# Two more weight slots for a mixture-of-experts kernel: the one-hot gate tables are replaced by pieces made expert by expert

## What is computed

```
aff   = softmax(h @ w_router)                 # 256 x 16
rows  = the 32 tokens with the largest aff[:, e]
g, u  = h[rows] @ w_gate[e], h[rows] @ w_up[e]    # 1024 x 1024 each
y     = (silu(g) * u) @ w_down[e]             # 1024 x 1024
x[rows] += gate_vector * aff[rows, e] * y
```

## Time and profile before

| | |
|---|---|
| median of 3 runs | 2050.88 us (2050.53 to 2053.23) |
| the profiled execution: its own time | 2045.0 us |
| its span, first to last instruction | 2043.2 us |
| mean granted TensorE clock | 0.893 |
| busy: PE, DVE, ACT | 83%, 28%, 20% |
| DMA: bytes moved, mean rate | 571.81 MB, 280 GB/s |
| expert part of layer 0, first gate_up to last scatter | about 1034 to 1490 us |
| expert part of layer 1 | about 1569 to 2025 us |

### The profile page before, as it was taken

The page is one execution under the profiler, slowest core; times in us unless marked ns, Lnnn a source line. Parts: engine busy times, 40 slices in busy tenths (PEclk is TensorE's granted clock), DMA queues, the critical chain, the costliest instruction groups (busy, mean ns, idle before and its releaser), DMA issues.

```text
span 2043.2 us, 22615 instructions
## 1 busy us (share of the span) xinstructions
PE 1702.8 (83%) x9278; PEld 1089.1 (53%) x9278; DVE 573.0 (28%) x1302; ACT 417.5 (20%) x732; POOL 18.5 (1%) x26
## 2 busy tenths in 40 slices
PE   6899989999999999996888777677687967766776
PEld 4544357887888886553744333343345624333433
DVE  3242145117888536546230000000024000000002
ACT  4222241002220023212221111111123211111111
POOL 0000000000110000000000000000000000000000
PEclk9999897999999999887868988888897878888888
DMA  9425730244558835105659999999985899999994
GB/s 365 174 78 206 292 124 1 83 165 173 201 182 329 309 111 202 41 6 202 250 236 402 429 427 429 427 430 427 425 317 214 337 429 428 429 428 430 427 430 199
DMA packets 110595, 571.81 MB, mean 280 GB/s; under 512 B 9121, under 2 KB 15393, under 8 KB 85954
## 3 DMA queue, kind: packets, MB, share of 16 engines
q1 hardware_dynamic: 109488, 568.66, 69.2%
q10 hardware_dynamic: 1042, 2.24, 0.3%
HBM read 569.83 MB, written 1.05 MB: 279 GB/s over the span
## 4 chain that ended last, share of the span: by engine, by line
PE 60%; DMA 30%; DVE 5%; ACT 2%; issue 2%; SPq 1%; DVEq 0%; ACTq 0%
DMA ring<-in_w_exp_up_dram 29%; PE bank L461 19%; PE bank L1105 10%; PE bank L805 8%; PE bank L832 4%; PE bank L469 3%; PE bank L487 2%; PE bank L848 1%; PE bank L1182 1%; PE bank L541 1%; PE bank L512 1%; PE bank L1124 1%; PE bank L1133 1%; PE bank L1091 1%; DMA ring<-in_w_ada_dram 1%
## 5 line engine op out<-in xcount | busy, mean ns | idle before, releaser
L1105 PE MATMUL bank<-ring,arena 128*32 128x512 f32 x1952 | 296.3, 755 | 217.0 <-DMA ring<-in_w_exp_up_dram 215.1
L1105 PEld LDWEIGHTS bank<-ring,arena 128*32 128x32 f32 x1952 | 80.6, 134 | 425.0 <-issue 422.3
L2350 DVE TENSOR_TENSOR arena<-arena,bank 128x256 f32<-128x256 f32 x32 | 13.5, 422 | 622.0 <-ACT arena L1630 622.0
L461 PE MATMUL bank<-ring,hT 128*128 128x512 f32 (+4 forms) x480 | 161.0, 492 | 6.5 <-issue 4.9
L805 PE MATMUL bank<-hT,ring 128*128 128x256 f32 x704 | 156.2, 384 | 4.2 <-ACT hT L1336 4.2
L805 PEld LDWEIGHTS bank<-hT,ring 128*128 128x128 f32 x704 | 135.2, 193 | 23.2 <-issue 4.6
L1124 PE MATMUL bank<-ring,arena 128*32 128x512 f32 x1024 | 129.2, 650 | 1.9 <-DVE arena L2350 1.9
L461 PEld LDWEIGHTS bank<-ring,hT 128*128 128x128 f32 x480 | 86.8, 192 | 75.8 <-issue 66.3
L1626 ACT COPY arena<-bank 128x512 f32<-128x512 f32 x32 | 33.5, 1046 | 444.8 <-PE bank L1105 444.8
L1133 PE MATMUL bank<-arena 128*128 (+1 forms) x512 | 119.1, 386 | 1.6 <-DVE arena L2354 1.6
L1133 PEld LDWEIGHTS bank<-arena 128*128 128x128 f32 x512 | 94.6, 190 | 41.1 <-issue 26.0
(11 more groups left out here) (311 smaller groups left out, 1718.6 us busy)
## 6 DMA issues: line engine op xcount, KB each, us to landing
ring<-in_w_exp_down_dram SPq DMA_DIRECT2D x64, 2048.0 KB, 17.6
ring<-in_w_exp_up_dram SPq DMA_DIRECT2D x62, 2048.0 KB, 23.3
ring<-in_w_exp_gate_dram SPq DMA_DIRECT2D x60, 2048.0 KB, 18.8
ring<-in_w_mod_dram SPq DMA_DIRECT2D x24, 2048.0 KB, 13.4
ring<-in_w_ada_dram SPq DMA_DIRECT2D x12, 2048.0 KB, 13.7
ring<-in_w_up_dram SPq DMA_DIRECT2D x10, 2048.0 KB, 11.4
ring<-in_w_in_dram SPq DMA_DIRECT2D x8, 2048.0 KB, 14.1
ring<-in_w_down_dram SPq DMA_DIRECT2D x5, 2048.0 KB, 9.3
```

Of the source, the lines that this page charges most:

```text
L461: ins = pe.matmul(b, lhs(k), rhs(k), start=(k == 0), stop=(k == n - 1))
L1105: ins = pe.matmul(bank[0][32 * q:32 * q + 32, :], xe[:, k * CAP:(k + 1) * CAP], xs[q // 2][:, o:o + 512], start=(k == 0), stop=(k == KD - ...
```

## The change

`EXTRA` becomes 5. The tables are gone: `hot` and `hotg` hold one expert, DVE makes them anew for each expert, PE transposes the gated piece per expert (`gate_rows`, two transposes into the bank of `down`), and DVE copies it to `gates`, one expert wide. The room that they give back (columns 10240 to 14336 of `arena`) takes piece (3,1). Piece (4,1) goes into the tile `hT`, the normed input of the layer, after the transposes of it into `h_tm` are done. `pT` and the scratch tiles move to other columns. The DVE loop over experts is written out instead of looped. At the last expert, `scatter(14)` stands behind `products(15)`.

```diff
-EXTRA = 3
+EXTRA = 5
...
-        extra = [spare, ar(2048, SLOT), ar(6144, SLOT)]
-        gates_flat = ar(10240, N_EXP * T)
-        hot = ar(14336, TB, N_EXP * CAP)
-        hotg = ar(15360, TB, N_EXP // 2 * 4 * CAP)
+        extra = [spare, ar(2048, SLOT), ar(6144, SLOT), ar(10240, SLOT), hT.rearrange("p k t -> p (k t)")]
+        hotg = ar(16640, TB, 4 * CAP)
+        gates = ar(16896, T)
+        hot = ar(17152, TB, CAP)
...
                 def rows(e):
 
+                    pe.wait_ge(sem("hot_ready"), e + (N_EXP * layer + 1))
...
+                def gate_rows(e):
+
+                    pe.wait_ge(sem("gated_hot"), e + (N_EXP * layer + 1))
+                    for tb in range(TB):
+                        ins = pe.transpose(bank[2][:, tb * 128:tb * 128 + 128], hotg[:, tb, :], ident)
+                    ins.then_inc(sem("gates_turned"), 1)
...
                 gate_up(0)
-                pe.wait_ge(sem("one_hot"), 2 * layer + 2)
-                for e2 in range(N_EXP // 2):
...
-                        ins = pe.transpose(b[:, m * 128:m * 128 + 128], hotg[:, tb, e * 128:e * 128 + 128], ident)
...
                 def expert(e):
                     products(e)
+                    gate_rows(e)
                     rows(e + 1)
                     down(e)
                     gate_up(e + 1)
-                    scatter(e)
+                    if not (isinstance(e, int) and e == N_EXP - 2):
+                        scatter(e)
...
                 products(N_EXP - 1)
+                scatter(N_EXP - 2)
+                gate_rows(N_EXP - 1)
                 down(N_EXP - 1)
...
                 for j in range(PIECES):
                     if j == extras_at:
-                        put_extra()
+                        extras_free()
+                        put_extra(range(EXTRA - 1))
                     ahead[j]()
                     put(j, 0, 0)
+                sp.wait_ge(done, G.number[("ht", layer, 3)])
+                put_extra([EXTRA - 1])
...
+                def hot_rows(e):
+                    if e:
+                        dve.wait_ge(sem("rows_selected"), N_EXP * layer + e)
                     for tb in range(TB):
+                        ins = dve.tensor_scalar(hot[:, tb, :], numbers, turn_of[:, tb, e:e + 1], None, ALU.is_equal)
+                    ins.then_inc(sem("hot_ready"), 1)
+
+                def gated_rows(e):
+                    if e:
+                        dve.wait_ge(sem("gates_turned"), N_EXP * layer + e)
+                    for tb in range(TB):
+                        ins = dve.tensor_scalar(hotg[:, tb, :].rearrange("p (q c) -> p q c", q=4),
+                                                numbers.unsqueeze(1).to_broadcast([128, 4, CAP]),
+                                                turn_of[:, tb, e:e + 1], aff[:, tb, e:e + 1], ALU.is_equal, ALU.mult)
+                    ins.then_inc(sem("gated_hot"), 1)
...
+                for e in range(N_EXP):
+                    dve.wait_ge(sem("gates_turned"), N_EXP * layer + e + 1)
+                    dve.tensor_copy(gates, bank[2][:, 0:T]).then_inc(sem("gates_ready"), 1)
+                    dve.wait_ge(sem("silu_ready"), N_EXP * layer + e + 1)
...
+                    if e + 1 < N_EXP:
+                        gated_rows(e + 1)
+                    if e + 2 < N_EXP:
+                        hot_rows(e + 2)
```

More of the change, by code:

```diff
@@ L397, in build @@
         u_tm = ar(0, TB, D)
[L398 removed]
+        pT = ar(14336, KD, T)
         eps, one = small[:, 0:1], small[:, 1:2]
@@ L1051, in experts @@
                                   skip_group_check=True), ("cs", layer))
-                pe.wait_ge(sem("one_hot"), 2 * layer + 1)
+                pe.wait_ge(sem("hot_ready"), N_EXP * layer + 1)
                 for j in range(4):
                     G.read(pe, ("ht", layer, j))
-                for b in range(RING):
+                for b in range(2 * RING):
                     G.drain(pe, b)
                 first, came = moe_first[layer], moe_sent[layer]
-                def part(v, start, n):
-                    return v[:, start:start + n] if isinstance(start, int) else v[:, bass.ds(start, n)]
                 def slot(j, e):
@@ L1134, in scatter @@
                                         dsb[:, n // 4, (n % 4) * 128:(n % 4) * 128 + 128],
[L1135 to L1138, removed]
+                                        gates, start=False, stop=False, skip_group_check=True)
+                        if last and n % 2:
+                            ins.then_inc(sem("scattered"), 1)
                 first_rows()
                 gate_up(0)
-                pe.wait_ge(sem("one_hot"), 2 * layer + 2)
-                for e2 in range(N_EXP // 2):
[L1144 to L1148, removed]
-                        ins = pe.transpose(b[:, m * 128:m * 128 + 128], hotg[:, tb, e * 128:e * 128 + 128], ident)
-                    G.close(ins, ("gT", layer, e2))
-                for e2 in range(N_EXP // 2):
-                    G.read(pe, ("gT", layer, e2))
                 for b in acc:
                     pe.matmul(b[:, 0:2], ones, nul, start=True, stop=False, skip_group_check=True)
-                moe_base[layer] = G.count
                 def expert(e):
                     products(e)
+                    gate_rows(e)
                     rows(e + 1)
@@ L1241, in used_up @@
                 else:
-                    sp.wait_ge(done, e * 3 + (moe_base[layer] + 2))
+                    sp.wait_ge(sem("down_done"), e + (N_EXP * layer + 1))
             def send_experts(layer, ahead, extras_at, extras_free):
@@ L1257, in put, with put_extra @@
                     load(ring[:, s * SLOT:(s + 1) * SLOT], j, e).then_inc(slot_full[s], 16)
-                def put_extra():
-                    extras_free()
-                    for j in range(EXTRA):
+                def put_extra(js):
+                    for j in js:
                         load(extra[j], j, 1).then_inc(extra_full[j], 16)
@@ L1627, in gate_and_up @@
                              bank[0].rearrange("p (c k) -> p c k", k=4)).then_inc(sem("gu_copied"), 1)
-                    act.wait_ge(done, e * 3 + (base + 1))
+                    act.wait_ge(sem("products_turned"), e + (N_EXP * layer + 1))
                     t = bank[1].rearrange("p (j c) -> p j c", j=4)
@@ L1633, in down_rows @@
                 def down_rows(e):
-                    act.wait_ge(done, e * 3 + (base + 2))
+                    act.wait_ge(sem("down_done"), e + (N_EXP * layer + 1))
                     act.copy(dsb[:, 1, :], bank[3]).then_inc(sem("down_copied"), 1)
@@ L2356, in experts @@
                 for n in range(KD):
-                    dve.wait_ge(done, base + 3 * (N_EXP - 1) + 3 + n // 2)
+                    dve.wait_ge(sem("scattered"), RING * layer + 1 + n // 2)
                     dve.scalar_tensor_tensor(xT[:, n, :], acc[n // 2][:, (n % 2) * T:(n % 2) * T + T], gate[:, n:n + 1],
```

71 lines of the change are left out of this document (22 added, 49 removed).

## The result

The changed kernel takes 2022.35 us (median of 4 runs, 2022.01 to 2022.59), the kernel before beside it 2050.70: a ratio of 0.9859, 95% interval 0.9842 to 0.9876, faster by 28.4 us. Predicted were 2020 us, in a range of 2013 to 2034, and -30.7 us.

A forecast was written before the change was run, and what follows sets the result against it. The prediction took the full DMA queue to bound the middle of each expert part. Two layers of -17.1 us shift and +1.75 us tail gave -30.7 us, so 2050.9 became 2020 us, range 2013 to 2034.

The forecast's parts named there:

- Bound: Middle of each expert part: a full DMA queue bounds it, 4.90 us a piece; only pieces remaining and earlier dry time count.
- Two pieces ahead: Before the first release: (3,1) and (4,1) are sent early, each worth 4.9 us, together 9.8 us.
- The start: First experts without gate tables: `down(0)` ends at 1054.2, `down(1)` at 1072.9, so (5,2) flows at 1073.8.
- A: Rival: clock stays at 2.4 GHz through the first experts, `down(0)` 2.0 us shorter, 2016 us; chance 0.12.
- B: Rival: half clock from 1044 on through `gate_up(1)`, shift 11.1 us, 2032 us; chance 0.12.
- The shift: Start of (5,2) in each layer: 1073.8 instead of 1090.9, so 17.1 us earlier, and everything behind it too.
- The tail: From the end of `gate_up(15)` to `down(15)`: 6.8 us instead of 5.05, costing 1.75 us a layer.
- Per expert at nothing: Each expert's added DVE instructions and 0.3 us of PE cost nothing, covered by the DMA queue.
- The clock: TensorE drops to half some 6 us after `gate_up(0)`: `rows` escapes, `down(0)` pays 5.48 us, `down(1)` takes 3.5.
- C: Rival: the two pieces come but the dry time does not shrink, 2035 us; chance 0.07.
- D: Rival: an extra waits longer for its tile and the tail takes back the gain, 2051 us; chance 0.04.
- E: Rival: mean clock in the middle falls below 0.64, PE becomes the bound, 2280 us at half clock; chance 0.05.

The follow-up runs named there:

- gates_24: The changed kernel with an expert's two gate transposes done 24 times over in experts 2 to 13 of each layer: 2020.1 us, ratio 0.9855.
- pieces_3: The changed kernel with EXTRA = 3, so pieces per expert but no slot more than before: 2033.5 us, ratio 0.9916.
- tables_4: The kernel before, with its gate tables, plus `hT` as a fourth extra sent after its transposes: 2050.4 us, ratio 0.9997.
- gates_72: The changed kernel with an expert's two gate transposes done 72 times over in experts 2 to 13 of each layer: 2145.9 us, ratio 1.0467.
- the last kernel: The changed kernel with (5,2) sent into tile `spare`, `scatter(14)` back ahead of `products(15)`, and five dense matmuls ahead of `gate_up(0)`: 2004.6 us, ratio 0.9787.
- tail_back: The changed kernel with `scatter(14)` moved back ahead of `products(15)`: 2018.7 us, ratio 0.9847.

## Why the prediction was right, step by step

- Bound. The queue bounds the middle and only its start counts: held. 29.37 us an expert in both kernels; `gates_24` hides 4.9 us of PE work for each.
- Two pieces ahead. Both are issued in time, the one for `hT` 16.8 us before the first release. But the split of the 17.1 us, 9.8 for the two pieces and 7.3 for the stall, is not one of cause: without the two slots (`pieces_3`) the changed kernel is 5.4 us a layer slower, not 9.8, and the pieces per expert alone bring 9.2. Alone, a slot can be worth nothing (`tables_4`). The 17.1 came out near because it was worked out from one event, the start of (5,2), and not from the two parts.
- The start. `down(0)` ended 10.8 us after `gate_up(0)`, 11.1 predicted. The clock fell once under `down(0)` as I had taken (5.22), so rivals A and B are out. It fell again under `down(1)` (5.27, where I had 3.5). This is the step that was mis-sized: (5,2) came 34.1 us after the first release instead of 33.2. In layer 1 `down(1)` did run at full clock (3.57), and `gate_up(0)` took 9.91 us instead. My remark that `gate_up(2)` releases four slots by 1080, before (5,2) has ended, doesn't follow from my own numbers, by which (5,2) ends at 1078.7; nothing hung on it, since its first half releases two slots sooner.
- The shift: at the second half of `gate_up(3)` 16.6 us in layer 0 and 17.2 in layer 1, 17.1 predicted.
- The tail: +1.3 us a layer, +1.75 predicted. The terms were each a little large: `scatter(14)` took 3.46 us from its start to that of `gate_rows(15)` (3.7 predicted), `products` 0.5 (0.6), the gates copy 0.35 up to `act_t` (0.42), and next to nothing was spent on handing over (0.2).
- Per expert at nothing: held. DVE's busy time in the middle doubled, from 13.36 to 27.73 us of 352, and no transfer waited. What the rule on grouping of the Trainium skill (Perfetto Trace Analysis, section Optimizing Scalar/DVE Operations) would have made of it, by the estimate in the prediction 9.6 us, is not there; the rule speaks of a saturated engine, and this one is not.
- The clock. I left open whether the pauses or the light work let it fall. In the changed kernel PE is busy without a pause from 1052 to beyond 1080, and the clock falls twice in it. Two windows of the second fall:

```profile
1072.00:1074.00 2.00, 2.00 (x20) 2.00 (x19) 0.71 (x3) 0.00 (x0) 0.00 (x0) 1.00 0.98 418
1076.00:1078.00 2.00, 2.00 (x16) 0.65 (x12) 0.00 (x0) 0.00 (x0) 0.00 (x0) 0.50 0.52 213
```

So a pause is not needed. What ran before each fall are the small matmuls of `products` and `rows`. `warm` fills waits with dense matmuls, and the clock is at full when `gate_up(0)` begins; it changes the pauses and the kind of work at once, so it does not tell which of them did it. The Trainium skill (TensorE: Matmul & The Clock Gate, section The HAM clock gate) says that activity releases the throttle. If activity is read as the busy time of the profile, the trace does not agree: the clock fell to 0.50 with PE busy for 2.00 of 2.00 us.
- Not in the prediction: +1.7 us between the layers, from the clock at the first matmuls there.
- The sum: the two layers gave -15.3 and -15.6, against -15.35 each. With the +1.7 it is -29.1 in the sum column, and -28.4 by runs. Carrying the profile's 5.9 us over to the median was right: "ahead" alone differed by 6.1 us between the profiles before and after. That layer 0 came out at the forecast's -15.3 is luck to half a microsecond: the shift was 0.5 us short and the tail 0.45 us cheaper, and the two errors cancel.

C, D and E did not happen. PE as the bound, which is what E is about, was made to happen in `gates_72`, by added work and not by the clock.

## What to carry to other kernels

In front of a stage that a full DMA queue bounds, work out for each transfer which release it waits for, and when the queue becomes full for good. A buffer more is worth its transfer only if it moves the last dry stretch; two that end on the same wait are worth no more than one. Before adding buffers, look for one that has been read and stands empty: a single reload of such a tile took 7 of the 43 us by which the first and the last kernel differ in the sum column. And when a piece of the work is moved behind the last transfer of such a stage, count it in full, since nothing hides it there: here it cost 1.2 us a layer, which `tail_back` gave back.

## What the runs showed of the hardware

TensorE's granted clock fell to 0.50 (1076 to 1078 us of the changed kernel) while PE had been busy in every one of the 2 us windows since 1052, first with matmuls of 32 moving columns (`rows`), and was back at full under the 128x512 matmuls of `down` and `gate_up`. The place of the fall is not fixed: the same `down(1)` took 5.27 us in layer 0 and 3.57 in layer 1 of one execution. Five dense matmuls of 0.9 to 2.0 us in PE's waits, whose result nobody reads, had `gate_up(0)` run at full clock in both layers (7.07 us instead of 9.25 and 9.91); `warm` took 2012.3 us against 2019.7 and 2022.35 of the changed kernel, and the intervals of the ratios lie apart. A full queue of 2 MB pieces moved 428 GB/s, 4.9 us a piece. The changed kernel reached `gate_up(0)` of layer 0 after 1034.2 us in one profile and after 1040.2 in the other; so a few us between two profiles mean nothing until the stretch in which they arise is known.
